# Gate/up projections of two feed-forward blocks by seven block products in place of eight

## What is computed

```python
def swiglu_ffn(h, w_gu, w_down):
    g, u = jnp.split(h @ w_gu, 2, axis=-1)
    return (jax.nn.silu(g) * u) @ w_down
for i in range(DEPTH):
    x = x + 0.5 * swiglu_ffn(rmsnorm(x, n_ffn1[i]), ffn1_w_gu[i], ffn1_w_down[i])
    ...
    x = x + 0.5 * swiglu_ffn(rmsnorm(x, n_ffn2[i]), ffn2_w_gu[i], ffn2_w_down[i])
```

## Time and profile before

| | us |
|---|---|
| time, median of 3 runs (lowest, highest) | 1993.27 (1992.75, 1993.96) |
| profiled execution: span from first to last instruction | 1992.3 |
| TensorE busy | 1983.5 (100%) |
| TensorE weight loads busy | 1654.4 (83%) |
| VectorE busy | 930.9 (47%) |
| ScalarE busy | 710.2 (36%) |
| GpSimd busy | 160.8 (8%) |

### The profile page before, as it was taken

The page is one execution under the profiler, slowest core; times in us unless marked ns, Lnnn a source line. Parts: engine busy times, 40 slices in busy tenths (PEclk is TensorE's granted clock), DMA queues, the critical chain, the costliest instruction groups (busy, mean ns, idle before and its releaser), DMA issues.

```text
span 1992.3 us, 23096 instructions
## 1 busy us (share of the span) xinstructions
PE 1983.5 (100%) x9182; PEld 1654.4 (83%) x9182; DVE 930.9 (47%) x1007; ACT 710.2 (36%) x865; POOL 160.8 (8%) x201
## 2 busy tenths in 40 slices
PE   9999999999999999999999999999999999999998
PEld 7888888888898888888888888888898888888887
DVE  5343443487865654434343443433287544434323
ACT  5222232256554543222222322222156443322222
POOL 2000001100112120000001000000112022200000
PEclk9999999999999999999999999999999999999999
DMA  5323352323434533232223323222353324432221
GB/s 176 105 88 102 100 142 76 104 64 106 129 126 127 169 106 106 84 105 88 96 95 100 106 84 105 87 98 95 121 165 114 103 85 127 158 105 96 94 95 74
DMA packets 204153, 214.53 MB, mean 108 GB/s; under 512 B 21970, under 2 KB 186960, under 8 KB 204096
## 3 DMA queue, kind: packets, MB, share of 16 engines
q1 hardware_dynamic: 180416, 192.95, 29.6%
q0 software_dynamic: 6432, 17.64, 3.4%
q10 hardware_dynamic: 17248, 3.16, 0.9%
HBM read 203.23 MB, written 10.49 MB: 107 GB/s over the span
## 4 chain that ended last, share of the span: by engine, by line
PE 96%; DVE 1%; DMA 1%; ACT 1%; issue 1%; SPq 0%; ACTq 0%; POOL 0%; DVEq 0%
PE ps L368 32%; PE ps L369 32%; PE ps L370 32%; DMA p_scratch<-sq 0%; ACT w_hi L1198 0%; DVE w_lo L1731 0%; DMA raw<-in_ffn_w_gu 0%; DVE sums L2213 0%; DMA p_tok<-p_scratch 0%; DVE sums L2233 0%; SPq L390 0%; DVE up L2411 0%; SPq L418 0%; PE ps L943 0%; PE ps L1138 0%
## 5 line engine op out<-in xcount | busy, mean ns | idle before, releaser
L368 PE MATMUL ps<-h_hi,w_hi 128*128 128x512 f32 (+1 forms) x1728 | 667.3, 386 | 0.2 <-DVE h_lo L1734 0.2
L369 PE MATMUL ps<-h_lo,w_hi 128*128 128x512 f32 (+1 forms) x1728 | 665.8, 385 | 0.0
L370 PE MATMUL ps<-h_hi,w_lo 128*128 128x512 f32 (+1 forms) x1728 | 665.8, 385 | 0.0
L1731 DVE TENSOR_TENSOR w_lo<-raw,w_hi 128x2048 fp32r<-128x2048 f32 (+4 forms) x195 | 417.4, 2141 | 461.8 <-ACT w_hi L1198 461.8
L1198 ACT ACTIVATE w_hi<-raw 128x2048 fp32r<-128x2048 f32 (+4 forms) x195 | 347.6, 1783 | 271.0 <-PE ps L370 266.9
L368 PEld LDWEIGHTS ps<-h_hi,w_hi 128*128 128x128 f32 x1728 | 324.7, 188 | 65.8 <-DVE h_lo L1734 0.9
L370 PEld LDWEIGHTS ps<-h_hi,w_lo 128*128 128x128 f32 x1728 | 324.6, 188 | 64.8
L369 PEld LDWEIGHTS ps<-h_lo,w_hi 128*128 128x128 f32 x1728 | 324.7, 188 | 64.0
L368 PE MATMUL ps<-mid_hi,w_hi 128*128 128x512 f32 x528 | 205.6, 389 | 0.0
L370 PE MATMUL ps<-mid_hi,w_lo 128*128 128x512 f32 x528 | 205.5, 389 | 0.0
L369 PE MATMUL ps<-mid_lo,w_hi 128*128 128x512 f32 x528 | 205.5, 389 | 0.0
(11 more groups left out here) (361 smaller groups left out, 1909.2 us busy)
## 6 DMA issues: line engine op xcount, KB each, us to landing
raw<-in_ffn_w_gu SPq DMA_DIRECT2D x87, 1024.0 KB, 5.1
raw<-in_ffn_w_down SPq DMA_DIRECT2D x34, 1024.0 KB, 4.9
raw<-in_x_w_kv SPq DMA_DIRECT2D x16, 1024.0 KB, 5.9
raw<-in_gla_w_in SPq DMA_DIRECT2D x12, 1024.0 KB, 5.1
raw<-in_ffn_w_down SPq DMA_DIRECT2D x12, 768.0 KB, 4.3
raw<-in_x_w_q SPq DMA_DIRECT2D x8, 1024.0 KB, 4.9
raw<-in_x_w_o SPq DMA_DIRECT2D x8, 1024.0 KB, 6.1
raw<-in_gla_w_out SPq DMA_DIRECT2D x8, 512.0 KB, 3.5
```

The source lines that it names most:

```text
L368: nc.tensor.matmul(out_ap, left[0], right[0], start=first, stop=False)
L369: nc.tensor.matmul(out_ap, left[0], right[1], start=False, stop=False)
L370: return nc.tensor.matmul(out_ap, left[1], right[0], start=False, stop=last)
L1731: return nc.vector.tensor_tensor(out_ap, value, hi.bitcast(F32), ALU.subtract)
```

## The change

In blocks n = 1 and 2 gate and up are computed together by a scheme of 7 products. The three split axes are the K rows (1024 as 2 x 512), the tokens (512 as 2 x 256), and gate against up (128 columns each). A slot now holds 128 gate and 128 up columns, by two loads. From it seven weight forms [128 x 4 x 128] are made: four are sums of quarters (GpSimd, `weight_sums`, from `raw` to `w_sums`), three are quarters; ScalarE and VectorE split each form. Likewise four sums of activation quarters are made once per block (`sum_x`, `scale_x`, `x_sums_hi`, `x_sums_lo`). Each product is 4 K chunks x 3 matmuls of 256 columns; sums of products are taken by accumulating in PSUM on banks that ScalarE or VectorE seeds with an earlier sum. Forms of a slot lie in one buffer of seven places; form i of the next slot may be written when product i is done. The first gate/up slot of each block (s = 0) stays as it was, now with gate and up columns.

The block runs in two halves of 11 slots: gate/up for 1408 mid columns, then the down projection over them (4 pairs, slots of 6 and 5 rows), added to x; then the same for the other half. Only the second half feeds the next norm. ScalarE and VectorE make the x sums and the first 3 or 4 forms between the steps of the pairs ahead of a block (`feed_last_pairs`), and the norm's `norm_roots` and `norm_inverses` come after these. ScalarE's `mixed_run` has the same order of steps as VectorE's, shown below: copy of the first product to the next bank (SEEDED), mid half, copy of the second (P5_TAKEN), forms 0 to 3 of the following slot, silu of the low half, forms 4 to 6, silu of the high half. `place` gives each slot a split buffer (`area`) of its own besides its raw buffer. The core of the diff (GpSimd's sums, TensorE's products, ScalarE's loop, VectorE's pairs ahead of a block, VectorE's loop):

```diff
+    MIXED = (1, 2)
+    HALF = FC // 2
+    HALF_GROUPS = ((0, 6), (6, 5))
+    KH, TH = C // 2, SEQ // 2
+    PRODUCTS = 7
+    SUM_OF = {1: 0, 2: 1, 4: 2, 6: 3}
+    X_SUM_OF = {1: 0, 2: 1, 4: 2, 5: 3}
...
+    def leading(w):
+        return 3 + (area[w] == 0)
...
+        def form_source(w, i):
+            if i in SUM_OF:
+                return w_sums[:, SUM_OF[i], :, :]
+            return quarter(w, int(i > 0), int(i == 5))
...
+                            for g in range(2):
+                                sp.dma_start(raw[:, w % 2, :, g * P:(g + 1) * P], both[:, :, g, s * P:(s + 1) * P])\
+                                  .then_inc(raw_loaded[w % 2], 16)
...
+            def weight_sums(n, part):
+                for m in range(mixed_first[n, part], mixed_end(n, part)):
+                    w = mixed_slots[m]
+                    pool.wait_ge(raw_loaded[w % 2], loaded[w])
+                    if m > 0:
+                        pool.wait_ge(*form_lo_count(m - 1, 1))
+                    nc.gpsimd.tensor_tensor(w_sums[:, 0], quarter(w, 0, 1), quarter(w, 0, 0), ALU.subtract)\
+                      .then_inc(sig.w_sum_ready, 1)
+                    if m > 0:
+                        pool.wait_ge(*form_lo_count(m - 1, 2))
+                    pool.wait_ge(sig.w_sum_ready, OPENED + 4 * m + 1)
+                    nc.gpsimd.tensor_tensor(w_sums[:, 1], quarter(w, 1, 1), w_sums[:, 0], ALU.subtract)\
+                      .then_inc(sig.w_sum_ready, 1)
+                    if m > 0:
+                        pool.wait_ge(*form_lo_count(m - 1, 4))
+                    nc.gpsimd.tensor_tensor(w_sums[:, 2], quarter(w, 1, 1), quarter(w, 0, 1), ALU.subtract)\
+                      .then_inc(sig.w_sum_ready, 1)
+                    if m > 0:
+                        pool.wait_ge(*form_lo_count(m - 1, 6))
+                    if m == mixed_first[n, 0]:
+                        pool.wait_ge(sig.x_sum_step, OPENED + 16 * (MIXED.index(n) + 1))
+                    pool.wait_ge(sig.w_sum_ready, OPENED + 4 * m + 2)
+                    nc.gpsimd.tensor_tensor(w_sums[:, 3], quarter(w, 1, 0), w_sums[:, 1], ALU.subtract)\
+                      .then_inc(sig.w_sum_ready, 1)
...
+            weight_sums(1, 0)
+            weight_sums(1, 1)
             add_squares(4)
+            weight_sums(2, 0)
+            weight_sums(2, 1)
...
+                for i, bank in enumerate((6, 7, b, 6, b, d, b)):
+                    if i < 6:
+                        pe.wait_ge(sig.form_lo_ready, count(6, OPENED + 6 * m + i + 1))
+                    else:
+                        pe.wait_ge(sig.w_lo_ready, count(1, w + 1))
+                    if i == 0 and m > 0:
+                        pe.wait_ge(sig.mixed_dve_step, count(6, dve_step(m - 1, C11_TAKEN)))
+                    if i == 1:
+                        if m > 0:
+                            pe.wait_ge(sig.mixed_act_step, count(3, act_step(m - 1, P5_TAKEN)))
+                        if (part, l) == (0, 0):
+                            pe.wait_ge(sig.x_sums_ready, OPENED + KH * (MIXED.index(n) + 1))
+                    if i == 2:
+                        pe.wait_ge(sig.mixed_act_step, count(3, act_step(m, SEEDED)))
+                    if i == 4:
+                        pe.wait_ge(sig.mixed_dve_step, count(6, dve_step(m, U4_SEEDED)))
+                    if i == 6:
+                        pe.wait_ge(sig.mixed_dve_step, count(6, dve_step(m, C22_READY)))
+                    hi, lo = form(w_hi, w, i), form(w_lo, w, i)
+                    for kk in range(KH):
+                        right_hi, right_lo = activation_form(i, kk)
+                        to, fresh = ps[:, bank, 0:TH], i < 2 and kk == 0
+                        nc.tensor.matmul(to, hi[:, kk, :], right_hi, start=fresh, stop=False, skip_group_check=True)
+                        nc.tensor.matmul(to, hi[:, kk, :], right_lo, start=False, stop=False, skip_group_check=True)
+                        last = nc.tensor.matmul(to, lo[:, kk, :], right_hi, start=False, stop=kk == KH - 1,
+                                                skip_group_check=True)
+                    last.then_inc(sig.product_done, 1)
...
+                if n in MIXED:
+                    project(("gu", n, 0), hh, feed=(None, 3, 4, 7)[n])
+                    for part in range(2):
+                        mixed_slot(n, part, 0)
+                        with pe.Fori(0, (mixed_count(n, part) - 1) // 2) as j:
+                            for l in (1, 2):
+                                mixed_slot(n, part, l, j)
+                        if part == 0:
+                            mixed_slot(n, part, mixed_count(n, part) - 1)
+                        half_down(n, part)
+                    return
...
+                    if l == 0:
+                        first = leading(mixed_slots[m])
+                        form_hi(m, first, sig.part_done, before_run)
+                        if part == 0:
+                            act.wait_ge(sig.evacuated, at["gu", n, 0].out + 1)
+                            nc.scalar.activation(t[:, 0, :], t[:, 0, :], ACT.Silu).then_inc(sig.silu_done, 1)
+                    act.wait_ge(sig.product_done, OPENED + PRODUCTS * m + 1)
+                    if l < 2:
+                        act.wait_ge(sig.evacuated, (o - 2 + 2 * l) if part == 0 else o - 1)
+                    if l >= 2:
+                        act.wait_ge(sig.mixed_dve_step, dve_step(m - 2, C21_TAKEN))
+                    nc.scalar.activation(ps[:, (even, odd)[l % 2], 0:TH], ps[:, 6, 0:TH], ACT.Copy)\
+                      .then_inc(sig.mixed_act_step, 1)
+                    if l == 0:
+                        for i in range(first + 1, PRODUCTS):
+                            form_hi(m, i, sig.part_done, before_run)
+                        if part == 0:
+                            act.wait_ge(sig.evacuated, at["gu", n, 0].out + 2)
+                            hi_part(half_hi[:, 0, :], t[:, 0, :]).then_inc(sig.mid_hi_ready, 1)
+                    else:
+                        low_mid_hi(s - 1)
+                    act.wait_ge(sig.product_done, OPENED + PRODUCTS * m + 2)
+                    if l >= 2:
+                        act.wait_ge(sig.mixed_dve_step, dve_step(m - 2, C22_READY))
+                    hi_part(sq[:, s % 2, TH:], ps[:, 7, 0:TH]).then_inc(sig.mixed_act_step, 1)
+                    following = m + 1 if m + 1 < end else None
+                    w = mixed_slots[m] + 1
+                    if following is not None:
+                        for i in range(4):
+                            form_hi(following, i, sig.product_done, OPENED + PRODUCTS * m + i + 1)
+                    else:
+                        split_hi(w % 2, area[w], loaded[w], OPENED + PRODUCTS * m + leading(w),
+                                 slot_rows[w], sig.product_done)
+                    act.wait_ge(sig.mixed_dve_step, dve_step(m, C11_TAKEN))
+                    nc.scalar.activation(t[:, s % 2, 0:TH], t[:, s % 2, 0:TH], ACT.Silu).then_inc(sig.mixed_act_step, 1)
+                    if following is not None:
+                        for i in range(4, PRODUCTS):
+                            form_hi(following, i, sig.product_done, OPENED + PRODUCTS * m + i + 1)
+                    act.wait_ge(sig.mixed_dve_step, dve_step(m, C21_TAKEN))
+                    nc.scalar.activation(t[:, s % 2, TH:], t[:, s % 2, TH:], ACT.Silu).then_inc(sig.silu_done, 1)
...
+            def feed_last_pairs(f, pair, split_after, residual):
+                if pair == 2:
+                    for m in (4, 5):
+                        residual(m)
+                        feed(f, m)
+                    sum_x(f, 0)
+                    split_next(split_after)
+                    x_sums_lo(f, 0)
+                    sum_x(f, 1)
+                else:
+                    m = mixed_slots.index(split_after + 2)
+                    residual(6)
+                    feed(f, 6)
+                    x_sums_lo(f, 1)
+                    residual(7)
+                    feed(f, 7)
+                    sum_x(f, 2)
+                    form_lo(m, 0)
+                    x_sums_lo(f, 2)
+                    sum_x(f, 3)
+                    form_lo(m, 1)
+                    x_sums_lo(f, 3)
+                    for i in range(2, leading(split_after + 2)):
+                        form_lo(m, i)
...
+                        gated_high(m - 1, s - 1)
+                        half_mid_lo(s - 1)
+                    if following is not None:
+                        form_lo(following, 0)
+                    dve.wait_ge(sig.product_done, OPENED + PRODUCTS * m + 3)
+                    dve.wait_ge(sig.mixed_act_step, act_step(m, P5_TAKEN))
+                    nc.vector.tensor_tensor(ps[:, d, 0:TH], ps[:, b, 0:TH], sq[:, s % 2, TH:], ALU.add)\
+                      .then_inc(sig.mixed_dve_step, 1)
+                    if following is not None:
+                        form_lo(following, 1)
```

(34 more changed lines are left out.)

343 lines of the change are left out of this document (315 added, 28 removed).

## The result

The changed kernel takes **2038.67 us** (median of 4 runs, 2036.80 to 2041.00) against 1993.05 (4 runs, 1992.75 to 1993.96): a ratio of **1.0228**, 95% interval 1.0214 to 1.0243. Forecast were 2032.5 us and a range of 2004 to 2056. The profiled execution spans 2036.6 us, 44.3 more than the one before.

What follows compares the result with a forecast made beforehand. TensorE, by the distance between matmul starts, was taken to bound the kernel. Terms -33.6 + 33.8 + 30.8 (entries) + 1.7 + 3.0 + 3.0 + 0.5 = +39.2 on 1993.3 gave 2032.5 us, range 2004 to 2056.

Steps and rivals of the forecast that it cites:

- mutual exclusion: GpSimd's sums and VectorE steps with both operands in SBUF: one waits until the other has finished; loop period 10.97 us.
- TensorE's own time: Gate/up slots of two blocks: 84 matmuls at 0.120 us, 10.08 us for 10.88 per slot, 42 slots: -33.6 us.
- The loop's waits: Steady slots: GpSimd's sums block VectorE, TensorE waits 0.89 us ahead of product 4, over 38 slots: +33.8 us.
- Loads: nothing, in either case: Weight loads of 1024 KB per slot, taking between 5.1 and 10.2 us, cost no time.
- Norm waits: Block entries: TensorE waits for the summed squares' split behind x sums and forms, 8.6 us second block, 9.5 third.
- Seed waits: Block entries: product 2 waits for ScalarE's seeding copy behind root and silu, 3.4 us in each block.
- U4 of the first slots: First slots of blocks: VectorE's step seeding the bank for product 4 comes late, costing 4.0 and 1.9 us.
- last down half: Third block's last down half: ScalarE's split for down pair 1 comes late behind memory norm work, +3.0 us.
- exits: Ends of gate/up halves: the other three cost 0.1 us each at the C12 bank; with later x stores +0.5.
- Clock: Long norm waits at the two entries lower TensorE's clock: 1.5 us each, +3.0 us.
- sums find gaps: Rival, 13%: GpSimd's sums slip under VectorE's PSUM steps and idle time; period 10.08 us, total 1988 us.
- Sums dearer: Rival, 10%: GpSimd's sums cost more in the loop; period 12 us, 73 us in place of 34, total 2071 us.

Runs made afterwards that it cites:

- run 4: Kernel with weight sums on VectorE (2004.02 us), the first sum moved into VectorE's idle 0.70 us, the second behind the step seeding product 4: 1992.05 us.
- run 1: Changed kernel with GpSimd's four weight subtractions per slot replaced by fills, then by copies, sums left out: fills 1985.23 us, copies 1993.73 us.
- run 2: Changed kernel with the mid half moved behind the C22 step on VectorE, and behind high form 1 on ScalarE: 2039.38 us.
- run 5: Changed kernel with the split of the summed squares for the norm put ahead of the last two x sums' low parts: 2033.09 us.
- run 8: Useless matmuls added where TensorE waits: changed kernel 2037.28 us; kernel with respaced sums on VectorE, early norm split and seed copy before silu 1988.14 us.

## Why the prediction was right, and where it wasn't

The total, the sign and the mechanism held: 2038.7 for 2032.5, because of a mutual exclusion read from two places of the trace before. The closeness of the total is in part luck: terms that were 12.2 us too small in the table stand against others 7.8 too large. By the steps:

- **TensorE's own time**: right; 0.120 us and 84 matmuls per slot, 10.08 where nothing else limits (run 4).
- **The loop's waits**: the period was forecast at 10.97 and is 10.97 to 11.1 in steady slots, and run 1 shows the cause. But the path to the number was partly wrong. I let sum 0 start when low form 1 of the slot before is done; it starts when its raw weights land (816.48, after 4.20 us of waiting), 2.1 us after that form's end at 814.36. So forms 1 to 3 are undisturbed, and 4, 5, 6 and the mid half are stretched, not 2, 3, 5 and the mid half. The period agrees because the price hardly depends on the place, in this kernel and in run 2; that it agrees to the hundredth is luck. The term was 2.3 too large: the last slot of each half has no next forms and no wait (4 x 0.89 counted in vain), while the second slots of the second halves wait 2.2 and 2.45 for late sums.
- **"Loads: nothing, in either case"** holds for TensorE, not for the step above: the load sets when GpSimd starts. Whether an earlier load would change the time wasn't tried.
- **Norm waits**: 12.9 and 11.6 for 8.6 and 9.5. Two things were missed. GpSimd goes on to the next slot's first two sums as soon as its buffer is free; in the third block they stretch three steps by 2.6 us together (1.69, 1.74, 1.75 for 1.23, 0.68, 0.69), in the second two by 1.5. And in the second block 2.2 us of pooling preparation stand in VectorE's queue ahead of the split. The reading that VectorE's queue up to the split is what TensorE waits for was right, and run 5 shows the larger truth: up to U4.
- **Seed waits**: 2.1 and 1.45 for 3.4. Product 2 was taken as due at full clock, 2.88 after the first matmul; at the lower one it is due later. What I forecast here shows as slow matmuls instead.
- **U4 of the first slots, last down half, exits**: 5.1 for 5.9, 2.3 for 3.0, 0.8 for 0.5.
- **Clock**: forecast 3.0, slow matmuls by the trace 6.9, but taking most of them away gave 1.4 (run 8). (By the earlier trace rows the clock fell 1.9 us behind the last matmul, not 1.6: full for 2.5 us, of which TensorE worked 0.6. Nothing rests on it.) Slow products run while VectorE's queue is being worked off. It must not be added to the waits; the table above does, as a count of where the time stood, not of causes.
- **The rivals**: "sums find gaps", 1988 us, is what run 1's fills nearly show (1985.2), so its arithmetic held and its condition failed. "Sums dearer" (1.9 us a slot) didn't happen: the four take 1.31 to 1.74 us.

From 2038.67 us, 34.7 come back by giving the sums to VectorE and 12.0 by the order of two of them. The reordered entries and the fillers give 0.9 and 3.0 in the times, 2.5 and 1.5 by the traces of the entries. The end is 1988.14 us, 0.24% under the kernel before, of the 1.7% that TensorE's own time would give. What remains is VectorE's work at the two entries, some 10 us each, which no reordering took away. A cheaper one (another reciprocal than the 3.35 us one, or x sums begun a pair earlier) wasn't tried.

## What to carry to other kernels

Before work is given to an idle GpSimd, look at what VectorE does in that stretch: if its steps have both operands in SBUF, the two take turns, and four sums of 0.60 us on VectorE cost less than four of 1.3 to 1.7 on GpSimd. A wait ahead of a stage is the length of the busiest other queue up to the last thing the stage needs; moving one step in that queue moves the wait, and only idle time in the queue can be won. Waits and slow matmuls behind them may be the same microseconds, so don't add them. And before a gain of a few us is put down to an edit, see in both traces that it lies where the edit is: more than half of run 8's 3.0 didn't.

## What the runs showed of the hardware

At the lower clock 256-column matmuls start 0.213 us apart, 1.8 times the 0.120 at the full one, and not twice. Fills on GpSimd (0.53 us for 512 elements) cost VectorE nothing; copies stretch a low form that they meet (0.83 for 0.68), and cost the loop nothing here. After one and the same wait of 2.09 us the granted clock was at the lower level in one run and at the full one in another (run 8). When both engines have SBUF operands, both are stretched: VectorE's 0.68 to as much as 1.78, GpSimd's 1.29 to as much as 2.24 (1130.87).
